# Layer norms, bank rotation, the experts' loop and the start of the third block in a three-block network on one core

## The chip, the cores and the metric

One Trainium2 chip, of which the kernel uses one core. The time is the device time of one launch, in microseconds (us). TensorE (PE) multiplies, VectorE (DVE), ScalarE (ACT) and GpSimd (POOL) do the element work, and SyncE (SP) issues most of the transfers from HBM.

## The reference

All tensors are float32, 256 tokens of 1024 features. The three blocks run one after another:

```python
# first block, twice (i = 0: SSD and short convolution; i = 1: window attention)
x = layer_norm(ALPHA * x + mix, ln_mix_g[i], ln_mix_b[i])
x = layer_norm(ALPHA * x + (silu(x @ w_gate) * (x @ w_up)) @ w_down, ln_ffn_g[i], ln_ffn_b[i])
x = x + (p[i] @ w_ple[i]) * sigmoid(x @ w_ple_gate[i] + b_ple_gate[i])
# second block: RWKV-7 and stick-breaking attention, then a mixture of 32 experts, 4 for each token
x = x + gate1 * mixed
h2 = rms_norm(x, norm2_g) * (1 + scale2) + shift2
x = x + gate2 * moe_ffn(h2, ...)     # one expert: (swiglu(xb @ w1[e] + b1[e]) @ w2[e] + b2[e]) * gate
# third block: latent attention and block attention, merged
h = rms_norm_3(x, g_pre) * (1 + scale) + shift
proj = h @ w_in
x = x + gate * rms_norm_3(y, g_post)
```

## The kernel before, in words

Activations lie with features on the partitions: `x_res` holds 8 tiles of 128 features by 256 tokens. `linear` (L326) runs a stream of weight panels through TensorE. A panel is 8 (or 6) tiles of 128 rows by 256 columns, 1 MB; SP loads it into one of six ring places (`issue_panels`, L237), and it gives a pair of output tiles. The tile programs of the engines are woven in: each yields the slot of the stream at which its next step is to run.

The two feed-forward networks of the first block go through `SevenProducts` (L524): a pair of panels' halves is multiplied with seven products of 128 x 128 instead of eight. One such product set of one panel is here called a **unit**; it is 28 matmuls of 128 columns (21 for a panel of six tiles), each done in two passes, so the profile counts 56 or 42. There are 66 units: in each of two layers 21 panels of the up projection (from its second pair on) and 12 of the down projection (4 pairs of 3 panels). A unit writes two PSUM banks: products 1, 6, 5 and 7 the first, products 2, 3 and 4 the second. For each unit POOL adds up weight tiles ahead (`sums`, L575, four operations; two buffers, so it starts when TensorE has left the unit before the last), ACT copies product 1 (L606) after product 6 is done, DVE combines in four steps (L612, L613, L615, and L618 after the last product), and `combined` is raised by L618. TensorE waits for its two banks at the start of a unit (`wait_bank`, L374). In this kernel the units use the bank sets (0, 1) and (2, 6) in turn (`SETS`, L529), and other pairs three banks in turn.

`LayerNorm` (L1085) is woven into the last projection ahead of it. Its steps: add up x of the first five tiles (L1168), one matmul with ones (L1127), subtract that mean from all (L1175 to L1180), square (ACT, L1148), add up the six squares on DVE (L1186), take tiles 6 and 7, three more matmul sums (L1130 to L1139), and then offset, variance, root, reciprocal (L1190 to L1199), and for each tile gain (DVE, L1204) and bias (ACT, L1157). The norms after the feed-forward networks are called `split`.

The experts' part (`mixture_of_experts`, L2745) first routes, in a block of its own, and then runs a loop over units of 64 tokens; in the profile there are 32, one for each expert. An expert's 12 panels are 6 pairs of 2 MB: pairs 0 to 3 are the wide matrix (L3071, two banks), pairs 4 and 5 the narrow one (L3101). `ExpertRing` (L3166) has 8 places: one for each pair, and a second for pairs 0 and 1 (`TWICE` = 2). `load_first` fills the 8 places before the routing. SP issues a later pair when TensorE has used the two panels in its place (`load`, L3020). TensorE's order in one turn: wide product of u (L3066, L3071), scatter of u-1 (L2831), gather for u+1 (L2803), narrow product of u. DVE adds what is scattered to `acc` (L2840). After the loop `ClosingNorm` (L2681) makes x and its root mean square, and the third block's `linear` begins with `NormTail` (L250), which scales and shifts the eight tiles of `h` before TensorE starts (L431).

## Time and profile before

| | |
|---|---|
| median of 3 runs | 2394.82 us (2394.03 to 2396.35) |
| time of the profiled execution | 2397.78 us |
| its span, first to last instruction | 2395.9 us |
| PE busy | 2261.8 us (94%) |
| DVE, ACT, POOL busy | 890.1, 419.3, 417.1 us |
| granted TensorE clock, mean | 0.987 |
| units of seven products | 275 to 481 us and 663 to 871 us |
| experts' loop | 1198 to 2117 us |
| third block | 2129 us to the end |

The span is read as a chain of stages. For each stage the question is which engine never waits. Where TensorE runs without a gap, what TensorE does sets the time; where the DMA engines are at their full rate throughout, the bytes do. A row of the timeline merges instructions of one kind that follow each other; "idle before" in brackets is the gap on that engine, with what ended it.

### The profile page before, as it was taken

What the parts mean: (1) busy time and instruction counts of PE and PEld (TensorE: products, weight loads), DVE (VectorE), ACT (ScalarE), POOL (GpSimd) and SP (SyncE); (2) the same over time, 40 slices, a digit from 0 to 9 for tenths busy, and PEclk for the clock granted to TensorE, in tenths of its full rate; (3) what the DMA queues carried; (4) which work ended last, traced back from release to release, by engine and by line L of the source; (5) the groups of instructions that cost most, each with busy time, mean ns of one, the idle gap of its engine ahead of it and who ended that gap; (6) DMA issues with size and microseconds to landing.
All of it is one profiled execution on the core that took longest, in us unless ns stands there. A gap on an engine that the chain in (4) does not pass through costs nothing. (4 is left out here: it accounts for less than half of the span.)

```text
span 2395.9 us, 35084 instructions
## 1 busy us (share of the span) xinstructions
PE 2261.8 (94%) x14543; PEld 1537.5 (64%) x14543; DVE 890.1 (37%) x1790; ACT 419.3 (18%) x898; POOL 417.1 (17%) x343
## 2 busy tenths in 40 slices
PE   8999999989899989999999999999999999989998
PEld 7888799977699977877733333333333333358886
DVE  4242565634444653626422222222322222253222
ACT  1210121014211013224111111111111111123331
POOL 0110498700088830011000000000000000000000
PEclk9999899999999989999999999999999999999999
DMA  6334644454854444310699999999999999943322
GB/s 263 132 124 141 213 167 160 163 191 181 317 211 161 160 170 154 124 37 2 283 376 428 428 428 428 428 428 428 428 428 428 428 428 428 428 194 124 143 71 88
DMA packets 61005, 619.28 MB, mean 258 GB/s; under 512 B 6784, under 2 KB 8064, under 8 KB 12288
## 3 DMA queue, kind: packets, MB, share of 16 engines
q1 hardware_dynamic: 59184, 611.08, 63.9%
q10 hardware_dynamic: 1712, 6.63, 0.8%
q8 instruction: 83, 1.36, 0.2%
q14 instruction: 26, 0.21, 0.0%
HBM read 616.63 MB, written 1.05 MB: 258 GB/s over the span
## 5 line engine op out<-in xcount | busy, mean ns | idle before, releaser
L431 PE MATMUL ps<-x_res,ring 128*128 128x256 f32 x1216 | 284.2, 393 | 24.0 <-ACT x_res L1157 15.4
L431 PEld LDWEIGHTS ps<-x_res,ring 128*128 128x128 f32 x1216 | 236.3, 197 | 64.8 <-issue 16.8
L3071 PE MATMUL ps<-expert_ring,moe_xg 128*64 128x512 f32 x1024 | 229.0, 594 | 25.7 <-DMA expert_ring<-we_dram 25.7
L3071 PE MATMUL ps<-ring,moe_xg 128*64 128x512 f32 x1024 | 227.9, 594 | 5.1 <-DMA ring<-we_dram 5.1
L3101 PE MATMUL ps<-expert_ring,mix_y 128*64 128x512 f32 x1024 | 226.8, 596 | 0.0
L3133 DVE TENSOR_SCALAR mix_y<-ps 128x512 f32<-128x512 f32 x32 | 22.1, 691 | 454.5 <-PE ps L3071 454.5
L3389 POOL COPY third_mla_kv<-third_lat 32x256 f32<-32x256 f32 x8 | 3.5, 457 | 1055.4 <-ACT third_mla_kv L658 1055.3
L3071 PEld LDWEIGHTS ps<-expert_ring,moe_xg 128*64 128x64 f32 x1024 | 71.5, 137 | 172.2 <-issue 124.6
L431 PE MATMUL ps<-third_h,ring 128*128 128x256 f32 x768 | 176.6, 387 | 5.2 <-ACT third_h L274 4.3
L3071 PEld LDWEIGHTS ps<-ring,moe_xg 128*64 128x64 f32 x1024 | 72.0, 137 | 150.9 <-issue 125.1
L431 PEld LDWEIGHTS ps<-third_h,ring 128*128 128x128 f32 x768 | 148.0, 194 | 28.1 <-issue 6.6
L3101 PEld LDWEIGHTS ps<-expert_ring,mix_y 128*64 128x64 f32 x1024 | 70.5, 137 | 133.4 <-issue 133.4
L3114 ACT ACTIVATE mix_y<-mix_y 128x512 f32<-128x512 f32 x32 | 20.2, 630 | 695.6 <-DVE mix_y L3133 695.6
L431 PE MATMUL ps<-mix_arena,ring 128*128 128x256 f32 x416 | 96.2, 389 | 4.3 <-ACT mix_arena L274 4.3
L586 POOL TENSOR_TENSOR ring<-ring 128x512 f32<-128x512 f32 (+1 forms) x66 | 99.9, 1514 | 0.0
L585 POOL TENSOR_TENSOR seven_weights<-ring 128x512 f32<-128x512 f32 (+1 forms) x66 | 86.0, 1304 | 71.8 <-PE ps L414 64.3
L431 PEld LDWEIGHTS ps<-mix_arena,ring 128*128 128x128 f32 x416 | 79.7, 194 | 17.3 <-issue 6.1
L588 POOL TENSOR_TENSOR seven_weights<-seven_weights,ring 128x512 f32<-128x512 f32 (+1 forms) x66 | 90.2, 1366 | 0.0
L414 PE MATMUL ps<-x_res,ring 128*128 128x128 f32 x672 | 89.0, 276 | 0.0
L414 PE MATMUL ps<-seven_x_turned,ring 128*128 128x128 f32 x672 | 88.8, 275 | 0.0
L414 PE MATMUL ps<-seven_x_turned,seven_weights 128*128 128x128 f32 x672 | 88.8, 275 | 0.0
L3148 DVE COPY moe_ytok<-ps 128x512 f32<-128x512 f32 x32 | 22.1, 692 | 176.1 <-PE ps L3101 176.1
(592 smaller groups left out, 3319.8 us busy)
## 6 DMA issues: line engine op xcount, KB each, us to landing
expert_ring<-we_dram SPq DMA_DIRECT2D x128, 2048.0 KB, 22.0
ring<-we_dram SPq DMA_DIRECT2D x64, 2048.0 KB, 24.5
ring<-w_in_dram SPq DMA_DIRECT2D x55, 1024.0 KB, 4.9
ring<-ffn_up_dram SPq DMA_DIRECT2D x44, 1024.0 KB, 4.9
ring<-ada_dram SPq DMA_DIRECT2D x36, 1024.0 KB, 4.9
ring<-w_out_dram SPq DMA_DIRECT2D x16, 1024.0 KB, 4.9
ring<-ffn_dn_dram SPq DMA_DIRECT2D x16, 1024.0 KB, 4.9
ring<-ple_g_dram SPq DMA_DIRECT2D x8, 1024.0 KB, 5.6
```

Source lines behind the costliest of these rows:

```text
L414: mm = pe.matmul(core.ps[:, bank, at:at + P], seven.weight(w, f, half, product, p), seven.moving(panel, sources[panel], k0, half, product, ...
L431: mm = pe.matmul(core.ps[:, bank_of[n, c], 0:TOK], w[:, k * PANEL + c * P:k * PANEL + c * P + P], sources[panel](k0 + k), start=(k0 + k == ...
L585: pool.tensor_tensor(s1, a21, a22, ALU.add).then_inc(summed.sem, 1)
L586: pool.tensor_tensor(a21, a11, a21, ALU.subtract).then_inc(summed.sem, 1)
L588: pool.tensor_tensor(s2, s1, a11, ALU.subtract).then_inc(summed.sem, 1)
L3071: mm = pe.matmul(ps[out, bank, :], xg[:, j % 4, j // 4, :], w[:, bank * D + at:bank * D + at + 512], start=False, stop=(j == 7))
L3101: mm = pe.matmul(ps[out, 2, :], hidt[:, at_k:at_k + S], w[:, i * D + at:i * D + at + 512], start=False, stop=(k == DT - 1))
L3114: act.activation(sg[:, :], glu[:, :], ACT.Sigmoid, scale=SWIGLU_ALPHA).then_inc(sig_ready.sem, 1)
L3133: dve.tensor_scalar(glu[:, :], ps[:, 0, :], SWIGLU_LIMIT, None, ALU.min).then_inc(glu_ready.sem, 1)
L3148: dve.tensor_copy(ytok[:, :], ps[:, 2, :]).then_inc(copied.sem, 1)
L3389: pool.tensor_copy(kv[64:96, t, :], lat[64:96, 3, :]).then_inc(*inc("keyed"))
```

## The change

It has five parts.

1. **Banks.** `SETS` is gone. Every pair and every unit takes its two banks from three in rotation by its number n: (2n) mod 3 and (2n+1) mod 3. So unit n+1 takes as its second bank the one that was the first bank of unit n. The wait at the start of a unit is the same code.
2. **Split norms.** The first mean is made of four tiles instead of five; x of tile 6 is no longer added on DVE (`add_last` only for the others), TensorE adds tiles 4 to 7 of x itself; the sum of six squares on DVE stands before the yield to tile 6, so ahead of the next unit's combination.
3. **Quiet.** POOL waits, before its first weight sums of each up projection, until the norm's eight gain operations on DVE are done.
4. **Experts' loop turned.** TensorE's program is cut into `widen` and `narrow`. `widen(0)` runs at the end of the routing block in place of twelve filler matmuls; the loop runs narrow(u), widen(u+1). Pair 2 has a second place as well (nine places, `TWICE` = 3), SP issues four loads in the routing block, and all six places of the ordinary ring are given back at once. `acc` is gone: DVE adds into x directly, eight operations of 256 columns instead of four of 512.
5. **Third block on raw tiles.** `UnscaledStart` replaces `ClosingNorm` and `NormTail`: TensorE multiplies x times gain with the first four output tiles, with the shift as a 257th column; DVE multiplies the products by the reciprocal root afterwards. The sum of squares is four matmuls between these products. `h` is made meanwhile for the later tiles.

```diff
@@ linear @@
-            bank = seven.SETS[n % 2][c] if seven is not None and pairs[q][0] in seven.names else (2 * q + c) % banks
+            bank = raw.BANKS[2 * q + c] if raw is not None and 2 * q + c < raw.COUNT else (2 * n + c) % banks
             bank_of[n, c], reused[n, c] = bank, user.get(bank)
             user[bank] = (n, c)
...
+                    if raw is not None and t < raw.COUNT:
+                        for m, k in enumerate(raw.ORDER):
+                            raw.before(pe, t, m)
+                            mm = pe.matmul(core.ps[:, bank_of[n, c], 0:raw.WIDTH], w[:, k * PANEL + c * P:k * PANEL + c * P + P], raw.moving(k),
+                                           start=(m == 0), stop=(m == DT - 1))
@@ SevenProducts @@
-    SETS = ((0, 1), (2, 6))
...
+        if core.stream[i][0:2] in self.quiet:
+            self.quiet[core.stream[i][0:2]](pool)
@@ LayerNorm.tensor @@
+        if self.split:
+            self.wait(pe, "centered", 2)
+            for t in range(4, 8):
+                if t == 6:
+                    self.wait(pe, "squares_added_up", 1)
+                    pe.matmul(ps[:, 5, 0:TOK], ones, self.run.shift[:, :], start=True, stop=False)
+                if t >= 6:
+                    core.wait_tile(pe, self.first + t)
+                mm = pe.matmul(ps[:, 4, TOK:], ones, x[:, t, :], start=(t == 4), stop=(t == 7))
+            mm.then_inc(*self.inc("mean"))
@@ LayerNorm.vector @@
+        summed = 4 if self.split else 5
+        for t in range(1, summed):
...
+        if self.split:
+            self.wait(dve, "squared", 2)
+            dve.tensor_reduce(run.shift[:, :], run.sq[:, 0:6, :].rearrange("p t n -> p n t"), AX,
+                              ALU.add).then_inc(*self.inc("squares_added_up"))
+        yield self.first + 6
+        if not self.split:
+            self.add_last(dve)
@@ first_block @@
+        for name, norm in (("ffn_up0", norms[0]), ("ffn_up1", norms[2])):
+            seven.quiet[name, 1] = lambda pool, norm=norm: norm.wait(pool, "scaled", DT)
@@ UnscaledStart @@
+    ORDER, BANKS, COUNT, WIDTH = (0, 1, 4, 5, 2, 3, 6, 7), (0, 1, 2, 6), 4, TOK + 1
...
+    def vector(self, dve):
+        for k in self.ORDER:
+            part = core.ps[:, 2 + k // 2, k % 2 * TOK:k % 2 * TOK + TOK]
+            dve.scalar_tensor_tensor(out=x[:, k, :], in0=part, scalar=gate[:, k:k + 1], in1=x[:, k, :], op0=ALU.mult,
+                                     op1=ALU.add).then_inc(*self.inc("kept"))
...
+    def scalar(self, act):
+        core.load_table(act, ACT.Sqrt)
+        for n, k in enumerate(self.ORDER):
+            self.at(act, "kept", n + 1)
+            act.activation(self.xg[:, k, 0:TOK], x[:, k, :], ACT.Copy, scale=core.gain[:, k:k + 1]).then_inc(*self.inc("gained"))
@@ mixture_of_experts @@
-                    keep_busy(12)
+                    widen(pe, 0, 0, 0)
...
+                with pe.Fori(0, last) as v:
+                    narrow(pe, v * 2, v, 0)
+                    widen(pe, v * 2 + 1, v, 1)
+                    narrow(pe, v * 2 + 1, v, 1)
+                    widen(pe, v * 2 + 2, v + 1, 0)
-PANELS, PAIRS, TWICE, AHEAD = 12, 6, 2, 9
+PANELS, PAIRS, TWICE, AHEAD = 12, 6, 3, 9
```

The rotation of the banks doesn't change the order: the names of the instructions and of the semaphores stay, only the count that TensorE waits for at a unit's start is higher by one. Three other places move.

On DVE, in the middle of the norm after the first feed-forward network (`x_res<-x_res,seven_stage 128x256` takes tiles 4 and 5, L618 or L638 is the last combination of a unit). Before:

```order
329 L618 TENSOR_TENSOR seven_stage<-seven_part,ps 128x384 [waits panel_used]
330 L1114 TENSOR_TENSOR x_res<-x_res,seven_stage 128x256 [waits seven_combined]
331 L1168 TENSOR_TENSOR ln_offset<-ln_offset,x_res 128x256 [waits dve_evac]
332 L1114 TENSOR_TENSOR x_res<-x_res,seven_stage 128x256 [waits seven_combined]
333 L1175 TENSOR_SCALAR ln_shift<-ps 128x256 [waits layer_signal28,dve_evac]
334 L1178 TENSOR_TENSOR x_res<-x_res,ln_shift 128x768 [waits dve_chain]
335 L1178 TENSOR_TENSOR x_res<-x_res,ln_shift 128x768
336 L1180 SCALAR_TENSOR_TENSOR x_res<-x_res,ln_shift 128x512
337 L612 TENSOR_TENSOR seven_second<-seven_part,ps 128x128 [waits seven_copied,dve_chain]
```

After:

```order
329 L638 TENSOR_TENSOR seven_stage<-seven_part,ps 128x384 [waits panel_used]
330 L1136 TENSOR_TENSOR x_res<-x_res,seven_stage 128x256 [waits seven_combined] x2
331 L1224 TENSOR_SCALAR ln_shift<-ps 128x256 [waits layer_signal28,dve_evac]
332 L1227 TENSOR_TENSOR x_res<-x_res,ln_shift 128x768 [waits dve_chain]
333 L1227 TENSOR_TENSOR x_res<-x_res,ln_shift 128x768
334 L1229 SCALAR_TENSOR_TENSOR x_res<-x_res,ln_shift 128x512
335 L1232 TENSOR_REDUCE ln_shift<-ln_sq 128x256 [waits layer_signal30,dve_chain]
336 L632 TENSOR_TENSOR seven_second<-seven_part,ps 128x128 [waits seven_copied]
```

The addition of tile 4 is gone, and the sum of squares, which waits for ACT, now stands ahead of the next unit's combination.

On TensorE, at the end of the routing block (L2907 to L2909 are the last matmuls of the routing). Before:

```order
1952 L2909 MATMUL ps<-route_onehot,mat 1x17
1953 L2870 MATMUL ps<-mat 128x128 [waits layer_signal26]
1954 L2870 MATMUL ps<-mat 128x128 x11
1955 L2858 UNCONDITIONAL_BRANCH
1956 L3050 UNCONDITIONAL_BRANCH [waits barrier_Pool_Activation_PE_DVE_SP_release]
```

After:

```order
1952 L3074 MATMUL ps<-route_onehot,mat 1x17
1953 L2949 MATMUL ps<-bias_parts,moe_pick 64x512 [waits layer_signal26,expert_xg_ready,expert_expert_picked]
1954 L2949 MATMUL ps<-bias_parts,moe_pick 64x512 x3
1955 L2954 MATMUL ps<-ring,moe_xg 64x512 [waits expert_pair0]
1956 L2954 MATMUL ps<-ring,moe_xg 64x512 x7
```

The first wide product stands ahead of the barrier between the two blocks instead of behind it.

On TensorE, from the last scatter to the third block. Before:

```order
2027 L2831 MATMUL ps<-moe_selt,moe_ytok 128x256 x7
2028 L2713 MATMUL ps<-moe_ht,mat 128x256 [waits stage_in] x8
2029 L3013 UNCONDITIONAL_BRANCH
2030 L391 UNCONDITIONAL_BRANCH [waits barrier_Pool_Activation_PE_DVE_SP_release]
2031 L431 MATMUL ps<-third_h,ring 128x256 [waits stage_end,panel_loaded0]
```

After:

```order
2090 L2929 MATMUL ps<-moe_selt,moe_ytok 128x256 x7
2091 L3177 UNCONDITIONAL_BRANCH
2092 L401 UNCONDITIONAL_BRANCH [waits barrier_Pool_Activation_PE_DVE_SP_release]
2093 L439 MATMUL ps<-unscaled_x,ring 128x257 [waits layer_signal42,layer_signal40,panel_loaded0]
2094 L439 MATMUL ps<-unscaled_x,ring 128x257 [waits layer_signal42] x7
2095 L439 MATMUL ps<-unscaled_x,ring 128x257 x4
2096 L2766 MATMUL ps<-unscaled_sq,mat 128x256 [waits layer_signal44]
```

The eight sums of squares are gone from before the barrier; four stand in the middle of the second output tile.

## Rows read from the trace of the kernel before

**Rows 1.** The page: the span; what the DMA engines moved, in 40 slices.

```profile
span 2395.9 us, 35084 instructions
...
GB/s 263 132 124 141 213 167 160 163 191 181 317 211 161 160 170 154 124 37 2 283 376 428 428 428 428 428 428 428 428 428 428 428 428 428 428 194 124 143 71 88
```

**Rows 2.** Windows: us, busy PE, PEld, DVE, ACT, POOL; PEclk, DMA share, GB/s.

```profile
275.00:481.00 206.00, 202.67 (x1796) 202.21 (x1794) 116.62 (x190) 31.69 (x62) 169.48 (x124) 0.99 0.48 165
...
1203.00:2117.00 914.00, 867.70 (x4330) 318.68 (x4326) 237.84 (x540) 98.21 (x145) 0.00 (x0) 1.00 1.01 427
```

**Rows 3.** Timeline, regular unit boundary: start, us, engine, line, op, count, [idle before].

```profile
350.11 1.06 PE L414 MATMUL ps<-x_res,ring 128*128 128x128 f32 x8
350.32 0.56 DVE L618 TENSOR_TENSOR seven_stage<-seven_part,ps 128x384 f32<-128x384 f32 x1 [1.01 <-PE ps L414]
```

**Rows 4.** Line L618 grouped: count, ns min/median/max, first and last start.

```profile
L618 DVE TENSOR_TENSOR seven_stage<-seven_part,ps x66: 546/554/556, 281.5 to 870.1; 128x384 f32<-128x384 f32 x66
```

**Rows 5.** Timeline: L618 on both sides of a turning of hidden tiles.

```profile
369.08 0.56 DVE L618 TENSOR_TENSOR seven_stage<-seven_part,ps 128x384 f32<-128x384 f32 x1 [1.24 <-PE ps L414]
...
378.35 0.55 DVE L618 TENSOR_TENSOR seven_stage<-seven_part,ps 128x384 f32<-128x384 f32 x1
```

**Rows 6.** Timeline, middle of the norm after the first feed-forward network.

```profile
460.86 0.70 PE L1127 MATMUL ps<-ln_offset,mat 128*128 128x256 f32 x2 [2.71 <-DVE ln_offset L1168]
...
461.39 1.77 PE L414 MATMUL ps<-first_arena,ring 128*128 128x128 f32 x8
...
469.48 0.56 DVE L618 TENSOR_TENSOR seven_stage<-seven_part,ps 128x384 f32<-128x384 f32 x1 [1.16 <-PE ps L414]
```

**Rows 7.** Timeline, end of the same norm.

```profile
480.42 0.56 DVE L618 TENSOR_TENSOR seven_stage<-seven_part,ps 128x384 f32<-128x384 f32 x1 [0.57 <-PE ps L414]
...
481.81 2.74 DVE L1186 TENSOR_REDUCE ln_shift<-ln_sq 128x256 f32<-128x1536 f32 x1
...
488.96 0.42 DVE L1190 TENSOR_SCALAR ln_offset<-ps 128x256 f32<-128x256 f32 x1 [4.08 <-PE ps L1137]
...
494.99 3.25 DVE L1204 SCALAR_TENSOR_TENSOR x_res<-x_res,vec,norm_rstd 128x256 f32<-128x256 f32 x8
```

**Rows 8.** Timeline, norm ahead of the first feed-forward network.

```profile
257.25 10.61 DVE L1204 SCALAR_TENSOR_TENSOR x_res<-x_res,vec,norm_rstd 128x256 f32<-128x256 f32 x8
...
258.69 0.67 PE L431 MATMUL ps<-x_res,ring 128*128 128x256 f32 x2 [3.48 <-ACT x_res L1157]
...
268.44 0.69 DVE L596 TENSOR_TENSOR seven_x_turned<-x_res 128x512 f32<-128x512 f32 x1 [0.57 <-ACT x_res L1157]
...
275.08 1.05 PE L414 MATMUL ps<-x_res,ring 128*128 128x128 f32 x8
```

**Rows 9.** Timeline, norm ahead of the second feed-forward network.

```profile
653.47 4.27 DVE L1204 SCALAR_TENSOR_TENSOR x_res<-x_res,vec,norm_rstd 128x256 f32<-128x256 f32 x8
```

**Rows 10.** A 3 us window before the experts' loop, columns as above.

```profile
1191.00:1194.00 3.00, 1.70 (x15) 1.39 (x14) 1.62 (x7) 0.60 (x1) 0.00 (x0) 1.00 0.54 229
```

**Rows 11.** Timeline, end of routing and the first expert.

```profile
1193.66 0.20 PE L2909 MATMUL ps<-route_onehot,mat 32*1 32x17 f32 x2
...
1198.02 1.28 ACT L3114 ACT_TABLE_LOAD   x1 [6.01 <-PEq L2858]
...
1198.37 0.62 PE L3066 MATMUL ps<-bias_parts,moe_pick 96*64 96x512 bf16 x4 [1.64 <-issue]
...
1202.63 7.20 SPq L3020 DMA_DIRECT2D ring<-we_dram  x3
```

**Rows 12.** Timeline, from the last expert to the third block.

```profile
2117.87 2.00 PE L2831 MATMUL ps<-moe_selt,moe_ytok 64*128 64x256 f32 x16 [0.87 <-DVE moe_ytok L3148]
...
2120.28 0.81 ACT L2705 ACTIVATE moe_ht<-x_res 128x256 f32<-128x256 f32 x2 [8.14 <-DVE x_res L2697]
...
2120.74 1.13 PE L2713 MATMUL ps<-moe_ht,mat 128*128 128x256 f32 x4 [0.87 <-ACT moe_ht L2705]
...
2130.68 19.18 PE L431 MATMUL ps<-third_h,ring 128*128 128x256 f32 x80 [4.26 <-ACT third_h L274]
```

## What the change was expected to do

> **What bounds the kernel now.** I read the page first. The span is 2395.9 us, and the profiled execution took 2397.78 us, 3.0 us above the median of 2394.82 us; sums are made against the execution and then laid on the median. The line of GB/s splits the program [rows 1]: DMA moves 428 GB/s for the whole of the experts' loop and less than half of that in the first block. The windows say the same in busy time [rows 2]. From 275 to 481 us, the first network of seven-product units, TensorE is busy 202.67 of 206.0 us at a clock of 0.99 (the 2.4 GHz level) with DMA at 0.48. So TensorE bounds it, and whatever it waits there is added to the end. From 1203 to 2117 us the DMA engines are at 1.01 and TensorE has 46 us to spare: there only bytes, and the moments at which the stream of bytes stops, count. The norms' ends and the two joints of the experts' part are chains from engine to engine.
>
> **1. Banks: the term that decides.** At a regular boundary TensorE begins unit n+1 at 350.11, and DVE's last combination of unit n runs from 350.32 to 350.88 [rows 3]. Before, this hurts nobody, since unit n+1 writes other banks. Afterwards the second bank of n+1 is the first bank of n, which L618 still reads; and TensorE asks for both banks at the unit's start, though it needs the second only for product 2. So its start moves to the end of L618 at the earliest: 0.77 us later, and 0.13 more for the step from a DVE result to the first product, an estimate from the nearest handover in the rows: the first of ACT's two squares ends at about 2120.69 and TensorE starts on it at 2120.74 [rows 12], 0.05 us, and I allow somewhat more for a DVE operation's end. I take **0.9 us a boundary**; its ends are 0.77 and 1.1. L618 is the same everywhere, 546 to 556 ns in 66 units [rows 4], so the price repeats. There are 66 units and 64 boundaries between them. Two already wait for DVE (the split norms' middles) and one, between up and down projection, has other matmuls that cover the wait. 61 x 0.9 = **+54.9** (47 to 67).
>
> In some units DVE turns hidden tiles and the combination comes late. Over such a place the L618 end at 369.64 and 378.90, 9.26 us apart [rows 5]. A unit takes about 6.3 us (1792 unit matmuls, nearly all of the 1796 in [rows 2], in 206.0 less the 3.2 us of the split middle), so a regular period would now be 7.2, and 2.1 us of this lateness reach TensorE. Four such places and two with 0.6: **+9.5** (6 to 12).
>
> **2. Split norms.** In the middle, TensorE idles 2.71 us for DVE's sum, does 0.53 us of matmuls and begins the unit at 461.39 [rows 6]: 3.24 us in all, of which 0.9 stay. Also the unit behind it ran slow: its combination ends at 470.04, 8.65 us after its start against 7.0 of a regular one (6.3 + 0.77), so 1.6 us went to a clock that had fallen. Both gains together 3.9. Against them, the sum of six squares, 2.74 us [rows 7], now stands ahead of that combination. From 8.65 take the 1.16 us that DVE waited for TensorE before L618 [rows 6], add 2.74, and add 1.0 for additions that TensorE no longer awaits: 11.2 us after the unit's start, where 7.2 would be in step. That is 4.0 us of a new stall. Net **0** for the two norms (-6 to +3).
>
> At the end, offset begins at 488.96, 8.0 us after the last combination ended at 480.98; in between are the 2.74 us and 4.08 us of waiting for the other sums [rows 7]. Left over are an addition, a square and one sum, about 1.8 us, an estimate from operations of 0.42 us and the handovers between. -6.2 x 2 = **-12.4** (the reduce alone, -5.5, to -13.5).
>
> Eight stalls of 2 to 4 us are new or longer than before. After a stall of 3.24 us the clock fell in the trace, at a cost of 1.6; I let this happen after the two of 4: **+3** (0 to 10).
>
> **3. Quiet.** The eight gain operations take 10.61 us ahead of the first network [rows 8], 4.27 ahead of the second [rows 9] and 3.25 in a norm where POOL adds nothing [rows 7]. With POOL silent I expect about 3.3. TensorE's first unit starts at 275.08 behind them, the turnings (L596, from 268.44) and the first pair [rows 8]. 7.3 us go directly, 2.0 more since TensorE, which starves at 258.69 for 3.48 us, runs that pair at the lower clock: **-9.3** (-6 to -10). Second network: **-1.0**. POOL's eight additions then fall on the turnings, which get slower, but these have the first pair's matmuls as cover. The Trainium skill, page "SBUF — State Buffer", section "SBUF: two separate sides", says that a DVE operation with two operands and a GpSimd one take the shared port pair in turn, each for its whole length; the row of 10.61 against 3.25 agrees. The same rule speaks against the change, for it only moves the collision; that is rival 5.
>
> **4. Experts.** The preloaded stream ends at about 1192.6 (DMA share 0.54 of a 3 us window [rows 10]) and starts again with the load issued at 1202.63, when TensorE, which began the first wide product at 1198.37, has used the first pair [rows 11]. That product now follows directly on the routing's last matmul at 1193.66, so that load goes out about 4.5 us earlier. One more pair of 2 MB lies ready, 4.9 us at 428 GB/s. The loop is bound by bytes, so both count: 9.4. Off that come 1.6 for TensorE's pause at the barrier, 1.64 [rows 11], now inside the stream, and 0.3 for the last addition. **-7.5** (-10 to 0: zero if the places come free late after the barrier). The eight smaller additions cost DVE time that it has (238 of 914 us busy [rows 2]).
>
> **5. Third block.** From the last scatter's end, 2119.87, to the first projection at 2130.68 are 10.8 us of additions, squares, sums, root and scaling [rows 12]. Now stand there a barrier (1.64), an ACT table load of 1.28 [rows 11] and little more: start about 2123.0, 7.7 earlier. Back come four sums of squares between the products, 1.1 us for four at L2713 [rows 12], and about as much for waits on the gains, which ACT delivers at 0.4 us a tile ([rows 12], 0.81 for two). **-5.5** (-8 to +1). If the four output tiles wait for the reciprocal root, the banks of later tiles are late; they are four, so nothing but the fifth tile can feel it.
>
> **Sum.** 54.9 + 9.5 + 0 + 3 = +67.4; -12.4 - 10.3 - 7.5 - 5.5 = -35.7; net **+31.7**. Execution 2429.5, median 2426.5: I say **2426 us**. A measurement tells 0.2% (4.8 us) from no change.
>
> **Rivals.**
> 1. *The wait on the bank doesn't bite*: L618 would be done when TensorE asks. For it speaks only that busy ends of matmuls are modelled; against it the L618 that starts 0.21 us after the next unit's first product in row after row. From the sum without the regular boundaries, -23.3 us, the price per boundary has to be under 0.38 us for a gain. Without any stall the late combinations and the middles' new stalls go too: -35.7 - 7.5 = -43, **2352**. Chance 4%, on the other side.
> 2. *About no change*: a stall of 0.3 to 0.45, so L618 half hidden. **2395**. 4%.
> 3. *The clock falls in all units*: 0.9 us in 7.2 without work, and every unit runs partly at the 1.2 GHz level. The one case of it in the trace cost 1.6 a unit; x 61 = +98, **2524**. Against it, around 1191 to 1194 TensorE is busy 1.70 of 3 us with the clock at 1.00 [rows 10]. 5%. The milder form, in which every late combination is followed by a slow unit (six more x 1.6), gives **2436**. 8%. The Trainium skill, page "TensorE: Matmul & The Clock Gate", section "Part 1: The HAM clock gate (the "warmup" mystery)", says that activity lifts the throttle and idleness brings it back; which of the two a short stall in each unit is, the rows of before don't show.
> 4. *The experts' gain doesn't come*, since the stream waits at the barrier for as long as it starts earlier: +7.5, **2434**. 10%.
> 5. *Quiet only moves the collision*: the turnings, with POOL's additions beside them, become the last thing that the first unit waits for. The gains took 3.3 times their quiet length; a like stretch of the turnings, half of it uncovered, costs 3 to 4 us: **2430**. 9%.
>
> **How the numbers follow.** My forecast 60%, the rivals 4, 4, 5, 8, 10 and 9%. The range takes in all but rivals 1, 2 and the far case of 3, and the bounds of the stall (47 to 67), the largest unknown: **2409 to 2446**. Faster 4%, same 4%, slower 92%.
>
> **What would show it.** Right: TensorE's row at each unit's start carries about 0.9 us of idle time released by L618's counterpart (now L638), the windows of both networks are 25 to 35 us longer with TensorE's busy time unchanged and the clock near 1. The middles show one idle of about 4 us behind the moved sum; offset follows the last combination by about 2 us; the gains take 3.3 us; the DMA gap before the loop shrinks from 11 to about 6 us; the third block's first product stands 3 us behind the last scatter. Wrong: idle times under 0.4 at the boundaries, a busy time of units that grows at a clock near 0.5, or a loop that no longer runs at 427 GB/s.

## The result and the profile after

| | before | after |
|---|---|---|
| median | 2394.43 us (2391.91 to 2396.35) | 2438.36 us (2437.31 to 2438.82) |
| ratio, 95% interval | | 1.0184 (1.0166 to 1.0201) |
| span of the profiled execution | 2395.9 us | 2436.7 us |
| granted TensorE clock, mean | 0.987 | 0.988 |

The change makes the kernel 44 us slower; 31.7 were forecast. The two profiled executions are 40.8 us apart, since that of before, 2397.78 us, lies 3 us above its median and that of after (2438.61 us) doesn't. Cut at the same events of both traces, these 40.8 us divide so (the forecast's terms put into the same stretches):

| stretch | before | after | difference | forecast |
|---|---|---|---|---|
| start to the first unit | 275.08 | 266.61 | -8.5 | -9.3 |
| first network, to its last combination | 205.89 | 241.62 | +35.7 | +33.7 |
| from there to the second network | 182.45 | 177.13 | -5.3 | -7.2 |
| second network | 207.21 | 242.30 | +35.1 | +33.7 |
| to the routing's last product | 323.06 | 315.45 | -7.6 | -6.2 |
| to the last scatter | 924.18 | 924.19 | 0.0 | -7.5 |
| last scatter to the end | 278.03 | 269.40 | -8.6 | -5.5 |

Windows over both networks and over the experts' loop in the kernel after (us; busy time of PE, PEld, DVE, ACT and POOL with counts; granted clock, DMA share, GB/s) answer to [rows 2]:

```profile
267.00:508.00 241.00, 210.52 (x1795) 205.08 (x1795) 115.06 (x190) 31.89 (x62) 172.05 (x128) 0.99 0.43 143
685.00:928.00 243.00, 213.27 (x1824) 206.86 (x1816) 106.37 (x189) 20.96 (x58) 165.61 (x128) 0.99 0.43 148
1251.00:2167.00 916.00, 865.59 (x4328) 320.80 (x4324) 262.46 (x672) 98.00 (x144) 0.00 (x0) 1.00 1.00 424
```

TensorE idled for 3.3 of 206 us in the first network before, in the middle of the split norm; it now idles for 30 of 241 us, and the mean clock stays at 0.99, the 2.4 GHz level.

**The boundary.** The timeline after (start, us, engine, line, operation, count, [idle before]) at a regular boundary answers to [rows 3]; L638 is the last combination, L424 the unit's matmuls:

```profile
360.87 0.56 DVE L638 TENSOR_TENSOR seven_stage<-seven_part,ps 128x384 f32<-128x384 f32 x1 [1.24 <-PE ps L424]
...
361.57 1.13 PE L424 MATMUL ps<-x_res,ring 128*128 128x128 f32 x8 [0.74 <-DVE seven_stage L638]
```

TensorE starts 0.15 us after L638 has ended. From start to start a unit takes 7.22 us, where it took 6.25. Stalls are given below from the start of a unit's last matmul to the start of the next unit's first one: that was 0.11 us at a regular boundary before and is 1.01 now. The page's fifth part, costliest groups after (busy, mean ns, idle before with releaser), adds it up; nothing of it was there before:

```profile
L424 PE MATMUL ps<-x_res,ring 128*128 128x128 f32 x672 | 91.8, 280 | 33.1 <-DVE seven_stage L638 33.1
```

For the down projections the group with `first_arena` has 27.1 us more, so 60.2 us of TensorE's idle time end with this one instruction.

**Middle and end of the split norm** (timeline after, DVE and PE; L1136 adds to x, L1227 and L1229 subtract the mean, L1232 is the sum of squares that was moved), against [rows 6, 7]:

```profile
481.48 2.48 DVE L1136 TENSOR_TENSOR x_res<-x_res,seven_stage 128x256 f32<-128x256 f32 x2
...
484.45 3.41 DVE L1227 TENSOR_TENSOR x_res<-x_res,ln_shift 128x768 f32<-128x768 f32 x2
487.78 0.68 DVE L1229 SCALAR_TENSOR_TENSOR x_res<-x_res,ln_shift 128x512 f32<-128x512 f32 x1
488.84 2.78 DVE L1232 TENSOR_REDUCE ln_shift<-ln_sq 128x256 f32<-128x1536 f32 x1 [0.38 <-ACT ln_sq L1186]
...
492.50 0.55 DVE L638 TENSOR_TENSOR seven_stage<-seven_part,ps 128x384 f32<-128x384 f32 x1
...
493.20 2.05 PE L424 MATMUL ps<-first_arena,ring 128*128 128x128 f32 x8 [5.12 <-DVE seven_stage L638]
...
507.68 0.56 DVE L638 TENSOR_TENSOR seven_stage<-seven_part,ps 128x384 f32<-128x384 f32 x1 [0.57 <-PE ps L424]
...
509.91 0.42 DVE L1239 TENSOR_SCALAR ln_offset<-ps 128x256 f32<-128x256 f32 x1 [0.89 <-PE ps L1159]
```

The end of the norm shrank from 8.0 to 1.7 us, as meant. The middle has 5.12 us of idle time (a stall of 5.39 us) that wasn't there, and the eight matmuls behind it take 2.05 us instead of 1.06: the clock had fallen. A window shows it:

```profile
493.00:497.00 4.00, 3.80 (x18) 3.83 (x19) 0.74 (x2) 0.00 (x0) 0.00 (x0) 0.50 0.02 4
```

**Quiet** (timeline after, against [rows 8]; L1253 gains, L616 and L617 turnings, L448 the first pair):

```profile
256.76 3.26 DVE L1253 SCALAR_TENSOR_TENSOR x_res<-x_res,vec,norm_rstd 128x256 f32<-128x256 f32 x8
...
257.94 8.83 PE L448 MATMUL ps<-x_res,ring 128*128 128x256 f32 x32 [3.22 <-ACT x_res L1195]
...
260.62 1.29 DVE L616 TENSOR_TENSOR seven_x_turned<-x_res 128x512 f32<-128x512 f32 x1 [0.60 <-ACT x_res L1195]
261.84 1.75 DVE L617 TENSOR_TENSOR seven_x_turned<-x_res 128x512 f32<-128x512 f32 x1
...
266.61 1.05 PE L424 MATMUL ps<-x_res,ring 128*128 128x128 f32 x8
```

The gains take 3.26 us, the turnings 1.3 to 1.8 each instead of 0.69, and TensorE doesn't see the latter.

**Experts** (timeline after, PE and SP's queue, against [rows 11]; L2954 is the wide product, L3001 the loads, L2929 the first scatter, L2993 the narrow product):

```profile
1235.40 3.55 PE L2901 MATMUL ps<-moe_ht,moe_sel 128*64 128x512 f32 x8 [0.64 <-DVE moe_sel L2880]
...
1243.22 1.07 PE L2949 MATMUL ps<-bias_parts,moe_pick 96*64 96x512 bf16 x4
1244.08 12.88 PE L2954 MATMUL ps<-ring,moe_xg 128*64 128x512 f32 x48
...
1250.14 7.20 SPq L3001 DMA_DIRECT2D ring<-we_dram  x3
...
1262.61 3.65 PE L2929 MATMUL ps<-moe_selt,moe_ytok 64*128 64x256 f32 x16 [2.22 <-issue]
```

The wide product does follow the routing at once, but its first load goes out 7.0 us behind the routing's last product. That is 1.8 us earlier than the 8.9 of before, and not 4.5. Windows over the stream (last two columns: DMA share, GB/s):

```profile
1244.00:1248.00 4.00, 4.00 (x12) 1.18 (x10) 1.15 (x7) 0.00 (x0) 0.00 (x0) 0.50 0.23 94
1248.00:1252.00 4.00, 4.00 (x18) 1.21 (x16) 0.00 (x0) 0.00 (x0) 0.00 (x0) 0.88 0.30 57
...
1272.00:1276.00 4.00, 4.00 (x22) 1.38 (x20) 0.87 (x5) 0.00 (x0) 0.00 (x0) 1.00 0.34 66
1732.00:1736.00 4.00, 4.00 (x22) 1.30 (x20) 0.11 (x2) 0.00 (x0) 0.00 (x0) 1.00 0.45 102
```

The stream pauses at its restart (with TensorE at a clock of 0.50), once more at 1272, and again at 1733 us. Before, the first was the only long pause: behind it no window of 4 us up to the last loads falls under 352 GB/s.

**Third block** (timeline after, against [rows 12]; L439 raw products, L2766 the four sums of squares, L448 the fifth tile):

```profile
2167.30 2.00 PE L2929 MATMUL ps<-moe_selt,moe_ytok 64*128 64x256 f32 x16 [0.87 <-DVE moe_ytok L3259]
2172.30 5.45 PE L439 MATMUL ps<-unscaled_x,ring 128*128 128x257 f32 x24 [3.00 <-ACT unscaled_x L2806]
2177.58 1.89 PE L2766 MATMUL ps<-unscaled_sq,mat 128*128 128x256 f32 x8
2179.31 8.85 PE L439 MATMUL ps<-unscaled_x,ring 128*128 128x257 f32 x40
2187.99 3.62 PE L448 MATMUL ps<-third_h,ring 128*128 128x256 f32 x16
```

The first product stands 3.0 us behind the scatter's end, the number of the forecast.

### The profile page after: what moved, and what is told of

Same layout as the page of the kernel before. It is cut to its first block and busy times, and to the rows that moved or that the text cites. A ratio compares the mean times of both kernels' runs of the same rounds, so it can differ in the third digit from the quotient of the medians.

```text
span 2436.7 us, 35144 instructions
## 1 busy us (share of the span) xinstructions
PE 2260.8 (93%) x14519; PEld 1539.5 (63%) x14519; DVE 902.0 (37%) x1914; ACT 419.7 (17%) x899; POOL 411.2 (17%) x343
## 5 line engine op out<-in xcount | busy, mean ns | idle before, releaser
L2954 PE MATMUL ps<-expert_ring,moe_xg 128*64 128x512 f32 x1280 | 283.4, 594 | 26.0 <-DMA expert_ring<-we_dram 25.8
L448 PE MATMUL ps<-x_res,ring 128*128 128x256 f32 x1216 | 276.5, 387 | 18.9 <-ACT x_res L1195 10.3
L448 PEld LDWEIGHTS ps<-x_res,ring 128*128 128x128 f32 x1216 | 234.2, 195 | 54.1 <-issue 14.0
L2993 PE MATMUL ps<-expert_ring,mix_y 128*64 128x512 f32 x1024 | 226.8, 596 | 0.0
L2954 PEld LDWEIGHTS ps<-expert_ring,moe_xg 128*64 128x64 f32 x1280 | 89.6, 137 | 209.5 <-issue 160.7
L2954 PE MATMUL ps<-ring,moe_xg 128*64 128x512 f32 x768 | 170.6, 600 | 0.2
L448 PE MATMUL ps<-third_h,ring 128*128 128x256 f32 x704 | 160.1, 383 | 1.3 <-DVE third_h L3738 1.0
L2993 PEld LDWEIGHTS ps<-expert_ring,mix_y 128*64 128x64 f32 x1024 | 70.6, 137 | 133.3 <-issue 133.3
L448 PEld LDWEIGHTS ps<-third_h,ring 128*128 128x128 f32 x704 | 134.2, 192 | 21.2 <-issue 2.2
L2954 PEld LDWEIGHTS ps<-ring,moe_xg 128*64 128x64 f32 x768 | 55.2, 139 | 106.8 <-issue 100.7
L424 PE MATMUL ps<-x_res,ring 128*128 128x128 f32 x672 | 91.8, 280 | 33.1 <-DVE seven_stage L638 33.1
L424 PEld LDWEIGHTS ps<-x_res,ring 128*128 128x128 f32 x672 | 81.7, 192 | 40.3 <-issue 40.2
L2939 DVE SCALAR_TENSOR_TENSOR x_res<-ps,modulations,x_res 128x256 f32<-128x256 f32 x256 | 102.9, 474 | 0.0
L424 PE MATMUL ps<-first_arena,ring 128*128 128x128 f32 x528 | 75.8, 287 | 27.1 <-DVE seven_stage L638 27.1
L448 PE MATMUL ps<-mix_arena,ring 128*128 128x256 f32 x416 | 95.6, 388 | 4.3 <-ACT mix_arena L274 4.3
L448 PEld LDWEIGHTS ps<-mix_arena,ring 128*128 128x128 f32 x416 | 79.4, 194 | 17.1 <-issue 6.1
L424 PE MATMUL ps<-seven_x_turned,seven_weights 128*128 128x128 f32 x672 | 88.8, 275 | 0.0
```

What stands on the lines that cost most here:

```text
L424: mm = pe.matmul(core.ps[:, bank, at:at + P], seven.weight(w, f, half, product, p), seven.moving(panel, sources[panel], k0, half, product, ...
L448: mm = pe.matmul(core.ps[:, bank_of[n, c], 0:TOK], w[:, k * PANEL + c * P:k * PANEL + c * P + P], sources[panel](k0 + k), start=(k0 + k == ...
L2939: ins = dve.scalar_tensor_tensor(out=x[:, k, :], in0=ps[:, 2 + 2 * i + q, t * TOK:t * TOK + TOK], scalar=gate[:, k:k + 1], in1=x[:, k, :], ...
L2954: mm = pe.matmul(ps[out, bank, :], xg[:, j % 4, j // 4, :], w[:, bank * D + at:bank * D + at + 512], start=False, stop=(j == 7))
L2993: mm = pe.matmul(ps[out, 2, :], hidt[:, at_k:at_k + S], w[:, i * D + at:i * D + at + 512], start=False, stop=(k == DT - 1))
```

## The experiments

Theory: TensorE pays for a bank that DVE still reads, because it asks for it at the unit's start; the repair of the norm adds one long stall for each split norm by the same wait. The rivals are named with each run. Stretches are those of the table above.

**Two bank sets again, `a_oldbanks`.**

```diff
-            bank = raw.BANKS[2 * q + c] if raw is not None and 2 * q + c < raw.COUNT else (2 * n + c) % banks
+            bank = raw.BANKS[2 * q + c] if raw is not None and 2 * q + c < raw.COUNT else (((0, 1), (2, 6))[n % 2][c] if seven is not None and pairs[q][0] in seven.names else (2 * q + c) % banks)
```

> The changed kernel with the units' two bank sets (0, 1) and (2, 6) of before; all else as changed. Theory (TensorE pays for the bank that is still being read): a regular boundary goes back from 1.01 to 0.11 us and a unit from 7.22 to 6.25 us, the two stalls of 5.4 us in the split norms' middle and the slow units behind them (8.5 and 8.9 us) vanish. 54 units of 6.25 and 8 of 4.69 a pair of layers, 400 us, against 484: -80 to -84, median about 2356 us. Rival (the units lost time for another cause, such as the moved sum of squares or POOL's wait): boundaries stay at 1.0 us and the time stays above 2420.

Measured: 2358.55 us, ratio to before 0.9838 (0.9822 to 0.9855); the networks took 201.33 and 202.62 us, 80.0 less than in the changed kernel. So 80 us hang on the banks, more than the change as a whole lost, and the other four parts gain together: the kernel is now 38 us faster than before. The middle of the split norm in this kernel (timeline):

```profile
456.31 1.06 PE L424 MATMUL ps<-first_arena,ring 128*128 128x128 f32 x8
...
461.83 0.55 DVE L638 TENSOR_TENSOR seven_stage<-seven_part,ps 128x384 f32<-128x384 f32 x1
...
462.56 0.65 PE L424 MATMUL ps<-first_arena,ring 128*128 128x128 f32 x4
```

L638 is 6.07 us late against the start of unit 31, ends 0.18 us before unit 32 starts, and no one waits for it.

**The rotation alone on the kernel before, `b_rot`.**

```diff
-            bank = seven.SETS[n % 2][c] if seven is not None and pairs[q][0] in seven.names else (2 * q + c) % banks
+            bank = (2 * n + c) % banks
```

> The kernel before with the rotation of three banks alone. Theory: 62 boundaries at 0.97 more and six late combinations, four at 1.1 and two at 0.6, +65 us, 2459 to 2460; the middles of the split norms stay as before (TensorE waits longer for the norm than for the bank). Rival (the stalls are paid only because the norm's repair filled DVE): under +50.

Measured: 2462.96 us, beside 2396.54 for the kernel before, 1.0274 (1.0256 to 1.0292): +66.4. The networks took 239.47 and 238.15 us, 64.5 more. A regular boundary in this kernel (timeline; L618 is again the last combination, L414 the unit's matmuls) is that of the changed one:

```profile
346.08 1.13 PE L414 MATMUL ps<-x_res,ring 128*128 128x128 f32 x8 [0.74 <-DVE seven_stage L618]
```

The rotation needs no other part of the change to cost this. In the changed kernel it costs the networks 15.5 us more, 80.0, and this difference stands in the middles of the split norms: there DVE's work that is late for the next unit (the moved sum of squares and what is ahead of it, see `a_redlate`) becomes a stall.

**Three banks, but the second asked for when it is needed, `a_late`.**

```diff
                     wait_bank(pe, n, 0)
-                    wait_bank(pe, n, 1)
...
                     for product in seven.ORDER:
+                        if product == 2:
+                            wait_bank(pe, n, 1)
```

> The changed kernel with three banks in rotation, but TensorE waits for a unit's second bank in front of product 2, the fifth of the seven, instead of at the unit's start. Theory (it is the place of the wait, not the number of banks): the bank is asked for 3.6 us after the start and is free 1.0 us after it, so regular and late boundaries cost nothing. In the split norms' middle the combination comes 5.3 us after the unit before has ended, so 1.6 us remain there, twice. About -78, 2361 us. Rival (three banks are too few as such): nothing moves but the place of the stall, from the start to product 2, and the time stays near 2438.

Measured: 2366.67 us, 0.987 (0.9854 to 0.9887). A boundary is again 0.11 us (timeline; the second row is the start of a unit whose predecessor's combination is 3.6 us late):

```profile
315.45 1.06 PE L425 MATMUL ps<-seven_x_turned,ring 128*128 128x128 f32 x8
316.35 1.06 PE L425 MATMUL ps<-x_res,ring 128*128 128x128 f32 x8
```

In this unit and the three others with such a combination, 0.2 to 0.35 us of waiting now stand in front of product 2, 1.3 us in all, where the theory had none. So three banks are enough; the place of the wait was the fault. The networks take 9.7 us more than in `a_oldbanks` (the medians are 8.1 apart); the other 8.4 stand in the middles of the norms, 4.2 us each instead of the 1.6 expected (timeline, unit 31 in front of product 2):

```profile
459.16 1.06 PE L425 MATMUL ps<-seven_h_turned,seven_weights 128*128 128x128 f32 x8
462.59 1.50 PE L425 MATMUL ps<-first_arena,ring 128*128 128x128 f32 x8 [2.37 <-DVE seven_stage L639]
463.88 1.91 PE L425 MATMUL ps<-first_arena,seven_weights 128*128 128x128 f32 x8
```

2.37 us of idle, and three products at the lower clock behind it (0.57 over 463 to 467 us), 1.50, 1.91 and 1.57 instead of 1.06. The expectation had left this clock out, and the combination ended 6.2 us behind the last product of the unit before, not 5.3.

**The sum of squares behind the combination, `a_redlate`** (in the changed kernel; the block of L1232 is run after unit 30 is kept):

```diff
-        if self.split:
-            self.wait(dve, "squared", 2)
-            dve.tensor_reduce(run.shift[:, :], run.sq[:, 0:6, :].rearrange("p t n -> p n t"), AX,
-                              ALU.add).then_inc(*self.inc("squares_added_up"))
...
                             seven.keep(eng, link, f, core.stream[panel])
+                            if core.stream[panel][0:3] in seven.between:
+                                seven.between[core.stream[panel][0:3]](eng)
```

> The changed kernel with one step of the split norm moved: the sum of six squares on DVE stands behind the combination of the unit after it (unit 30 of 33) instead of ahead. Theory: the stall of 5.4 us at the start of unit 31 becomes a regular one of 1.0, and the unit behind it runs at the full clock, 6.2 instead of 8.5 and 8.9 us; -4.4 -2.5 twice, -13 to -14, 2425 us; the norm's end stays as it is, 1.7 us from the last combination to the offset. Rival (the combination is late for the additions of x, not for the sum): a stall of over 3 us stays, gain under 5.

Measured: 2430.11 us, 1.0148 (1.0128 to 1.0168); the networks took 8.5 us less than in the changed kernel, not 13. The stall in the middle fell from 5.39 to 2.88 us, start of product to start, in both norms (timeline):

```profile
489.13 0.55 DVE L641 TENSOR_TENSOR seven_stage<-seven_part,ps 128x384 f32<-128x384 f32 x1
...
489.83 1.40 PE L424 MATMUL ps<-first_arena,ring 128*128 128x128 f32 x5 [2.61 <-DVE seven_stage L641]
```

So the moved sum is 2.5 us of the 4.4 us that were more than a regular boundary. The other 1.9 us stay when the sum is gone; what then stands on DVE ahead of the combination are the additions of x and the subtraction of the mean (2.48 and 3.41 us in the rows of after). No run moves these. The clock took 2.3 and 2.65 us behind 5.39 us, and 1.4 and 0 behind 2.88. Neither theory nor rival was right in its number.

**The repair of the norms alone, on the kernel before, `b_split`** (all of part 2 of the change, nothing else).

> The kernel before with the repair of the split norms alone (mean of four tiles, TensorE adds tiles 4 to 7, sum of squares ahead of the next combination), two bank sets as before. Theory: with two sets the late combination of unit 30 (6.1 us behind the start of unit 31) stops nobody; the middles lose their 3.5 and 3.9 us of waiting and the slow unit behind (1.6, 1.3), the ends go from 8.0 to 1.7 us each. -9 -12.6, with up to 3 us of clock behind the second norm: -22 to -25, about 2372 us. Rival (the moved sum of squares costs what it costs in the changed kernel, 5 us and a slow unit each time): -8, about 2387.

Measured: 2371.13 us beside 2396.1, 0.989 (0.9869 to 0.9912): -25. The networks took 201.33 and 202.62 us, to the hundredth those of `a_oldbanks`. With two bank sets the repair is a gain of 25 us; its stall exists with the rotation only.

**Quiet alone, on the kernel before, `b_quiet`.**

```diff
+        if core.stream[i][0:2] in self.quiet:
+            self.quiet[core.stream[i][0:2]](pool)
```

> The kernel before with POOL's wait for the eight gain operations alone. Theory: ahead of the first network the gains go from 10.6 to 3.3 us and the first unit starts 8.5 us earlier; ahead of the second nothing comes of it (0 to +1, by the clock of the first pair). -7 to -9, about 2387 us. Rival (the collision only moves to the turnings, which then hold up the first unit): under -4.

Measured: 2387.66 us beside 2396.1, 0.9963 (0.9946 to 0.9979). The theory holds: the first unit starts at 266.64 us, 8.4 earlier, and the stretch between the networks is 1.3 us longer. Gains and turnings in this kernel (timeline):

```profile
256.80 3.26 DVE L1207 SCALAR_TENSOR_TENSOR x_res<-x_res,vec,norm_rstd 128x256 f32<-128x256 f32 x8
260.65 1.29 DVE L599 TENSOR_TENSOR seven_x_turned<-x_res 128x512 f32<-128x512 f32 x1 [0.60 <-ACT x_res L1160]
```

**Eight places instead of nine, `a_twice2`.**

```diff
-PANELS, PAIRS, TWICE, AHEAD = 12, 6, 3, 9
+PANELS, PAIRS, TWICE, AHEAD = 12, 6, 2, 9
```

> The changed kernel with eight places again, pair 2 has no second one. Theory: the ninth place saves a pair's 4.9 us of stream and loses 2.2 to the pause at the change of order, so without it the stretch from the routing's last product to the last scatter is 2.7 longer, 926.9 us. Rival (a place more is worth its bytes): 4.9 longer, 929.1 us. Second rival (the places don't bound it): unchanged, 924.2.

Measured: 2438.49 us, 1.0172 (1.0149 to 1.0194). The stretch from routing to last scatter is 924.4 us, unchanged, but 1.1 us stand in its favour, since its first load came 5.9 instead of 7.0 us behind the routing. From the first load to the last scatter it is 918.5 against 917.2. The ninth place is worth 1.3 us here, less even than theory said. The pause at 1733 us is absent.

**The second order of loads from the start, `a_inturn`.** In `in_turn` an odd unit's single places are loaded ahead of the next unit's double ones (pairs 0 to 2 have two places each, pairs 3 to 5 a single one).

```diff
-                with sp.Fori(2, AHEAD) as v:
-                    load(sp, v * 2 - 2, twice, 0, v * 2)
-                    load(sp, v * 2 - 2, once, 1, v * 2 - 1)
-                    load(sp, v * 2 - 1, twice, 1, v * 2 + 1)
-                    load(sp, v * 2 - 1, once, 0, v * 2)
...
-                with sp.Fori(AHEAD, E // 2 - 1) as v:
+                with sp.Fori(2, E // 2 - 1) as v:
```

> The changed kernel whose loads of the experts' pairs go in the second of the two orders (an odd unit's single places first) from the third pair of units on, instead of from the ninth. Theory: the change of order costs a pause of 2.2 us of the stream at 1733 us once, since the third double place leaves one load less in flight there; without the change of order it is gone, and the stretch from the routing's last product to the last scatter goes from 924.2 to 922 us. Rival (the second order pauses the stream wherever it begins): the pause stands near 1300 us and the stretch stays at 924.

Measured: 2447.98 us, 1.0202 (1.0177 to 1.0227). The rival is right, and more so: the pause stands at 1316 to 1332 us and is longer. From the first load to the last scatter 925.1 us, 7.9 more than in the changed kernel. Windows of this kernel:

```profile
1316.00:1320.00 4.00, 4.00 (x20) 1.28 (x18) 0.00 (x0) 0.00 (x0) 0.00 (x0) 1.00 0.13 53
...
1328.00:1332.00 4.00, 4.00 (x22) 1.43 (x20) 1.23 (x6) 0.00 (x0) 0.00 (x0) 1.00 0.16 33
```

**The first order for all units, with two bank sets, `o_first_b`.**

```diff
-                    load(sp, v * 2 - 2, once, 1, before)
                     load(sp, v * 2 - 2, twice, 0, even)
-                    load(sp, v * 2 - 1, once, 0, even)
+                    load(sp, v * 2 - 2, once, 1, before)
                     load(sp, v * 2 - 1, twice, 1, odd)
+                    load(sp, v * 2 - 1, once, 0, even)
```

> The changed kernel with the two bank sets of before, and with the first of the two orders of loads (double places first) for all pairs of units. Theory (the pause of 2 us at the ninth pair comes of the change of order): it is gone, the stretch from the first load to the last scatter goes from 916.8 us (changed kernel with two bank sets) to 914.6, and the median from 2358.5 to about 2356. Rival (the first order leaves the last expert's single pairs too late, since they are queued behind double ones): the stretch grows by 2 to 5 us at its end.

Measured: 2369.99 us, 0.988 (0.9862 to 0.9899), 11 us slower than `a_oldbanks`. The pause is gone, as theory said:

```profile
1732.00:1736.00 4.00, 4.00 (x26) 1.98 (x26) 2.62 (x4) 0.89 (x2) 0.00 (x0) 1.00 1.01 430
```

But the rival decides: the last expert's three single pairs are issued from 2055.58 us on, in `a_oldbanks` from 2044.28 on (SP's queue, L3001 in either kernel, here and, with the load before them in one row, there):

```profile
2055.58 13.79 SPq L3001 DMA_DIRECT2D expert_ring<-we_dram  x3
```

```profile
2030.11 27.97 SPq L3001 DMA_DIRECT2D expert_ring<-we_dram  x4
```

The stretch is 9.7 us longer, twice what the rival had said at most. The change of order costs a pause of 2 us and saves some 12 at the end.

**Fillers against the fallen clock, `o_first_fill_b`, `o_fill` and `o_fill_twice2`.** `o_fill` is `a_oldbanks` with:

```diff
-                    keep_busy(14)
+                    keep_busy(17)
                     pe.wait_ge(members.sem, members.at(1))
...
-                    keep_busy(4)
+                    keep_busy(7)
                     pe.wait_ge(copied_ht.sem, copied_ht.at(4))
```

> As the kernel with two bank sets and the first order of loads for all units, and six more filler matmuls on TensorE in the routing block, three ahead of each of two waits. Theory (the clock falls there by the idle time of TensorE): the granted clock stays at 2.4 GHz until the first expert, whose first pair takes 4.0 us instead of 5 to 6, so that the first load of the loop stands 5 us behind the routing's last product instead of 5.9 to 7.1; 1 to 3 us off the end, about 2354 us. Rival (the fall depends on when the clock is looked at, not on these fillers): the distance is again anywhere from 5.8 to 7.1 us.

> The changed kernel with the two bank sets of before and six more filler matmuls in the routing block, three ahead of each of two waits; orders of loads as changed. Theory: the clock stays up through routing and the first wide product, the first load of the loop stands 5.0 to 5.9 us behind the routing's last product and the fifth 12.3 instead of 13.9 us behind the fourth; 1 to 3 us less than with two bank sets alone, 2356 us, and the stretch from the first load to the last scatter 915 us. Rival (the clock's fall came from when it is looked at): no gain over 2358.5.

> The kernel just named with eight places instead of nine. Theory (the ninth place saves 4.9 us of stream and gives back some 2 at the change of order and some 1 to 2 elsewhere): the stretch from the first load to the last scatter is 1 to 3 us longer, 917 us, and the time 1 to 3 us above the nine places'. Rival (worth its bytes): 5 us above.

Measured: 2365.57 us against 2369.99 without fillers (first order of loads); 2356.64 us, 0.9833 (0.9818 to 0.9847), the fastest of all, and 2359.97, 0.9841 (0.9824 to 0.9857), with eight places. With fillers the gather of the routing (L2901) takes 1.94 us in all three profiles; without them it takes 1.94 us in `a_oldbanks`, `a_redlate` and `a_twice2`, but 3.5 to 3.6 in the changed kernel, `a_late`, `a_inturn` and `o_first_b`, which is too mixed to credit the fillers with it. The first load comes 5.9 us behind the routing in all three; so it does in the three without where the gather is fast (5.8 to 5.9), and 7.0 to 7.2 us behind it in the four where the gather is slow. Whether `o_fill` beats `a_oldbanks` (2356.64 and 2358.55) isn't settled: the intervals overlap. The ninth place: 914.7 against 918.3 us from first load to last scatter, of which 1.6 are a first scatter at the lower clock in the one (3.63 instead of 2.00 us); 2 us for the place.

## Why the prediction was right, and where it missed

Right: slower, and by the regular boundary above all. That the sum came as near as 9 us of the 40.8 between the traces is in part luck: the boundaries were 4 us dearer than forecast and the late combinations 4 us cheaper, and of the experts' 7.5 us that didn't come the third block's start gave back 3.

Three readings of the prediction were wrong without changing its sum. The first block moves 263 and 317 GB/s in two of its slices [rows 1], which is more than half of 428. The one boundary that has other matmuls as cover isn't between up and down projection but behind the first unit of the second network; those around the start of the down projections wait like all others. And the DMA gap before the loop did shrink from 11 to 6 us, as its signs said, but that is no sign of the gain: both terms of the experts' sum together, 9.4 us, would have left 1.7.

- **Boundary.** 0.9 us forecast, 0.97 measured (7.22 against 6.25). The handover from L638 to TensorE takes 0.15 us, for which 0.13 had been taken; 0.07 more is the first product (1.13 instead of 1.06 us), whose first weight load starts 0.03 us ahead of it where it was 0.11. 61 boundaries make 59 instead of 54.9. Rivals 1 and 2 fall, by `a_oldbanks` and `b_rot`.
- **Late combinations.** The step of 2.1 us was too large: 1.09 in four units and 0.54 in two, 5.4 instead of 9.5 in all. It took the 9.26 us between two combinations [rows 5] for fixed work. It isn't: POOL, which waits for TensorE's units, starts its sums later now, and DVE's last turning runs alone. Before, POOL's next sum began at 375.44 us, ahead of the turning of 375.81; after, at 382.67 us, with the turning of 382.06 all but done. The fourth turning before and after (timelines; L601 and L621 are the same operation):

```profile
375.81 1.65 DVE L601 TENSOR_TENSOR seven_h_turned<-first_arena,seven_h_turned 128x512 f32<-128x512 f32 x1
```

```profile
382.06 0.69 DVE L621 TENSOR_TENSOR seven_h_turned<-first_arena,seven_h_turned 128x512 f32<-128x512 f32 x1
```

- **Middles.** Net 0 was forecast with a combination 11.2 us behind the unit's start; it ended 11.5 us behind it (493.05 after 481.59). What was mis-sized is the clock: 3 us for both, 4.9 measured (units of 8.50 and 8.86 us instead of 6.21). Against before, the middles cost 2.6 and 3.0 us more: 5.6 instead of 3.
- **Ends.** 6.2 forecast, 6.3 measured, each. Behind the second, the next 48 matmuls ran in 10.60 us instead of 13.45, at the higher clock, 2.9 us that belong to no part of the change.
- **Quiet.** 8.5 instead of 9.3 ahead of the first network. Ahead of the second the gains fell from 4.27 to 3.25 us as forecast, and still the first unit came 0.9 later relative to them: the 32 matmuls of the first pair took 8.72 us, 7.8 before. Rival 5 didn't happen: the turnings became slow and stayed covered, in the changed kernel (first unit at 266.61 us) as in `b_quiet` (266.64).
- **Experts: the step that failed.** 7.5 us were forecast, nothing came, which is rival 4 in its sum, though by another road: not one wait at the barrier but three losses. The first load came 1.8 us earlier relative to the routing instead of 4.5, since the first 16 wide matmuls took 6.1 us and not 3.8, at the 1.2 GHz level (0.50 over 1244 to 1248 us). Between the fourth and fifth load lie 14.0 us where 9.9 were: the first narrow product waits for barrier, first scatter and gather, and the loads in flight (four pairs, 19.6 us of stream) run out, 4 us of pause. The pause at the change of order is 2 us. That is 2.7 + 4.1 + 2 = 8.8 of the 9.4 us of gain that the sum started from. For pauses the sum had allowed 1.6 us; these two are 6.1. `a_twice2` shows it for the ninth place: without it the time is the same, and one of the pauses, that at 1733 us, is gone. No run turns the loop back alone; the other two losses are read from the two traces.
- **Third block.** 5.5 forecast, 8.6 measured. The start was right: 5.0 us from the last scatter's start to the first product, 12.8 before, so 7.8 gained, and the same in each of the ten kernels that have the new start. The five first tiles took 19.15 us here, with 1.7 of sums in them, against 19.0 before, where the clock was 0.58 over their first 4 us (2130 to 2134 us). That gave back the 2.2 us that had been set against the gain, but it is chance: in the other nine kernels with the new start the whole stretch to the end takes 269.4 to 273.1 us, and the clock is low there in some (0.65 over 2169 to 2173 us in `a_twice2`). The last 1.0 us, further on, belongs to no part: `b_rot` and `b_split`, with the old start, have it too. By the medians of ten and of four kernels, 271.1 and 277.9, the part is worth some 6.8 us. No run isolates it.
- **Clock.** Rival 3 in its far form is refuted: units with a stall of 1.0 us in 7.2 run at 0.99. In the near form, too: behind the six late combinations (stalls of 1.6 and 2.1 us) units took 6.21 us, as everywhere. Slow units are seen only behind idle times of 2.4 us and more, and not behind each (below).

The Trainium skill, page "SBUF — State Buffer", section "SBUF: two separate sides", was cited for taking turns of DVE and GpSimd at a shared port pair. The rows of gains (3.26 for 10.61 us) and turnings (0.69 or 1.65 us, by whether POOL's operations run beside) agree.

## What to carry to other kernels

When buffers are saved by letting a user reuse one that its forerunner is still read from, ask for each buffer where it is first written, not at the start of the whole step: here this gives back 72 of the 80 us, with the same three banks. A chain that ends late (the moved sum of squares) is free as long as nobody waits for it, so changes have to be costed together: the repair of the norms gains 25 us alone, and beside the rotation its late sum becomes a stall. For a stream that is bound by bytes, count its pauses in the trace and not only the places: the ninth one was worth 1.3 to 2 us here, not its 4.9 us of bytes.

## What the runs showed of the hardware

- The granted clock fell in like places of like kernels or not. (A unit's time is given here from its first matmul's start to its last one's, 6.14 to 6.21 us at the 2.4 GHz level.) Behind a stall of 2.88 us the next unit took 7.62 us in one norm of `a_redlate` and 6.21 in the other; behind 3.96 us in `b_rot` 7.77 and 6.14. The gather of the routing, the same eight matmuls behind the same work, took 3.55 us in the changed kernel and 1.94 in `a_oldbanks`. Like stages so differ by 1 to 3 us without a difference in the code that would account for it, which is to be kept in mind before such a difference is explained; a stall of 5.39 us was followed by 2.3 to 2.65 us of loss both times.
- One DVE operation of 512 columns took 0.69 us alone and up to 1.76 us beside POOL's additions; eight gains 3.25 and 10.61 us.
- A DVE result reached a waiting TensorE in 0.15 us at 57 boundaries, regular and late, and in 0.26 at the six around the start of the down projections.
